# Expert rows turned by VectorE instead of TensorE, and loaded tile by tile from ScalarE's queue

## The reference, cut to what matters

```python
# h: (512, 1024), modulated RMSNorm of the residual stream; 16 experts, two per token
scores = sigmoid(h @ router_w)
# one group of 4 experts by the biased scores, then the top 2 inside it
for e in range(16):
    he = silu(h @ w1[e]) * (h @ w3[e])       # (., 512)
    out = out + gate[:, e:e + 1] * (he @ w2[e])
```

## Time and profile before

| | us |
|---|---|
| median of 3 runs | 1632.22 |
| lowest, highest | 1629.7, 1632.82 |
| the profiled execution, its own time | 1630.77 |
| its span in the profile | 1629.2 |
| first up part starts | 1313.63 |
| last down part over, about | 1601 |

### The profile page before, as it was taken

How to read it: one execution, slowest core, us unless ns; L and a number is a source line. 1 busy time by engine, 2 the same in 40 slices (tenths; PEclk the granted TensorE clock), 3 DMA queues, 4 the chain that set the end, 5 groups by cost and what they waited for, 6 DMA issues and landing times.

```text
span 1629.2 us, 25590 instructions
## 1 busy us (share of the span) xinstructions
PE 1537.2 (94%) x10014; PEld 1045.9 (64%) x10015; DVE 880.8 (54%) x1476; ACT 395.5 (24%) x736; POOL 311.5 (19%) x315
## 2 busy tenths in 40 slices
PE   5999999999999999999999999999999999999792
PEld 2567567567566788887755558888774665555351
DVE  2557848758758898763277765563362312222124
ACT  4342432432432410001133325101201201111112
POOL 0206516417417400000000000000000032222122
PEclk9999999999999999999999999999999989999996
DMA  9803401411411377131101102132637379998984
GB/s 339 330 11 77 126 17 39 129 26 28 128 52 36 147 255 254 60 105 52 52 1 52 52 1 103 54 121 103 241 121 258 132 268 395 376 351 323 395 325 168
DMA packets 110349, 248.61 MB, mean 153 GB/s; under 512 B 5665, under 2 KB 15142, under 8 KB 110274
## 3 DMA queue, kind: packets, MB, share of 16 engines
q1 hardware_dynamic: 86800, 180.60, 30.8%
q0 software_dynamic: 14288, 48.96, 8.4%
q10 hardware_dynamic: 9186, 18.01, 4.1%
HBM read 225.40 MB, written 22.15 MB: 152 GB/s over the span
## 4 chain that ended last, share of the span: by engine, by line
PE 80%; DVE 11%; DMA 4%; issue 1%; ACT 1%; SPq 1%; POOL 0%; ACTq 0%; DVEq 0%; POOLq 0%
PE psum L581 26%; PE psum L1273 9%; PE psum L513 8%; PE psum L1298 5%; PE psum L517 3%; PE psum L527 3%; PE psum L694 2%; PE psum L1089 2%; PE psum L971 2%; PE psum L853 1%; DMA arena<-exp_w_d 1%; PE psum L828 1%; DVE arena L2395 1%; DVE arena L2173 1%; PE psum L819 1%
## 5 line engine op out<-in xcount | busy, mean ns | idle before, releaser
L581 PE MATMUL psum<-arena 128*128 128x256 f32 x2128 | 472.4, 380 | 5.4 <-DVE arena L2063 2.1
L581 PEld LDWEIGHTS psum<-arena 128*128 128x128 f32 x2128 | 400.0, 190 | 73.9 <-issue 17.9
L1273 PE MATMUL psum<-arena 128*32 128x256 f32 x2816 | 165.9, 388 | 1.5 <-issue 1.0
L513 PE MATMUL psum<-arena 128*128 128x512 f32 x320 | 140.4, 592 | 0.0
L1273 PEld LDWEIGHTS psum<-arena 128*32 128x32 f32 x2816 | 89.9, 111 | 62.1 <-issue 7.3
L513 PEld LDWEIGHTS psum<-arena 128*128 128x128 f32 x320 | 59.2, 189 | 69.6 <-issue 69.3
L1991 DVE SCALAR_TENSOR_TENSOR arena<-arena 128x772 f32<-128x772 f32 (+1 forms) x96 | 101.9, 1062 | 3.4
L2773 DVE TENSOR_TENSOR arena<-arena,psum 128x128 f32<-128x128 f32 x44 | 12.7, 289 | 163.8 <-ACT arena L1829 163.8
L2880 POOL TENSOR_TENSOR arena<-arena 128x512 f32<-128x512 f32 x64 | 89.2, 1402 | 17.0 <-ACT arena L1603 16.8
L2941 POOL DMA_DIRECT2D slots<-arena x92 | 50.0, 545 | 196.8 <-DVE arena L2779 176.5
L2864 POOL TENSOR_TENSOR arena<-arena 128x512 f32<-128x512 f32 x32 | 45.1, 1410 | 216.7 <-ACT arena L1541 216.7
(11 more groups left out here) (402 smaller groups left out, 2152.5 us busy)
## 6 DMA issues: line engine op xcount, KB each, us to landing
arena<-exp_w_d SPq DMA_DIRECT2D x48, 2048.0 KB, 16.9
arena<-w_in_d SPq DMA_DIRECT2D x22, 2048.0 KB, 8.0
arena<-ada_w_d POOLq DMA_DIRECT2D x8, 2048.0 KB, 8.6
slots<-arena POOLq DMA_DIRECT2D x1, 9216.0 KB, 27.0
arena<-ada_w_d SPq DMA_DIRECT2D x4, 2048.0 KB, 20.7
arena<-decay_rows ACTq DMA_DIRECT2D x16, 512.0 KB, 6.8
arena<-ssd_proj_d SPq DMA_DIRECT2D x4, 2048.0 KB, 7.8
slots<-arena POOLq DMA_DIRECT2D x92, 64.0 KB, 5.0
```

Source lines behind the costliest of these rows:

```text
L513: ins = mmul(ps[:, 0:T], slot[:, k, m * P:(m + 1) * P], src[:, k, C:NT], start=(k == 0), stop=(k == KD - 1))
L581: ins = mmul(bank((name, at))[:, i * 256:(i + 1) * 256], held[:, k, i * P:(i + 1) * P], passed[:, k, :], start=(p in (1, 5, 6) and i == 0 ...
L1273: ins = mmul(psU[q * R:(q + 1) * R, 0:2 * HF], XT[:, k % 2, k // 2, :], w13[p][:, :, k, q * HF:(q + 1) * HF], start=(k == 0), stop=(k == K ...
```

## The change

Four things change together.

1. The rows of a tile are kept in quarters: row r's channels lie in four partition groups of 32, so that a transpose of 32x32 blocks by VectorE turns them. ScalarE writes `yo` in a reordered channel order, and `up` reads its weights in the matching order. `turn_x` and `turn_h` of TensorE and ScalarE's copy to `heT` go away; VectorE does `take_x` (transpose and scale), `give_x` (shift into `XT`) and `turn_h` (transpose into `heT`).
2. TensorE picks four tiles instead of two, not turned any more: `pick_x(psX, marks)` for tiles 0 and 1, and after `up(0, 0)` `pick_x(psX2, marks2)` for tiles 2 and 3. VectorE makes `marks2` from both choices of a token.
3. The loads of rows move from GpSimd (two tiles in one DMA) to ScalarE's queue: four DMAs of 32 KB a tile, after the previous tile's rows have landed and VectorE has taken a tile. SP loads tile 4, ahead of the last piece of expert 2's weights.
4. TensorE's order in a tile is up(j), down(j-1), and up(j) waits for he_ready itself.

```diff
-            def pick_x():
...
-                for k in range(KD):
+            def pick_x(rows, where):
+
+                for n in range(2):
                     for t in range(TL):
-                        ins = mmul(by_tile[:, :, k % 2, :, k // 2], yo[:, t, k * P:(k + 1) * P],
-                                   marks[:, t, :].rearrange("p (n r) -> p n r", n=2),
-                                   start=(k == 0 and t == 0), stop=(k == KD - 1 and t == TL - 1))
-                ins.then_inc(S_("x_turned"), 1)
-
-            def turn_x():
-                for i in range(DQ // P):
-                    ins = nc.tensor.transpose(psX[:, i * P:(i + 1) * P], xq[:, i * P:(i + 1) * P], ident)
-                ins.then_inc(S_("x_turned"), 1)
+                        for q in range(NQ):
+                            ins = mmul(rows[q * R:(q + 1) * R, n * DQ:(n + 1) * DQ], where[:, t, n * R:(n + 1) * R],
+                                       yo[:, t, q * DQ:(q + 1) * DQ], start=(t == 0), stop=(t == TL - 1))
+                    ins.then_inc(S_("x_picked"), 1)
 
             def up(p, j):
 
+                if not (isinstance(j, int) and j == 0):
+                    pe.wait_ge(S_("he_ready"), j)
+                    pe.sem_inc(S_("pe_passed"), 1)
                 pe.wait_ge(S_("x_ready"), j + 1)
...
-                pe.wait_ge(S_("xq_ready"), j + 2)
-                pe.sem_inc(S_("pe_passed"), 1)
-                turn_x()
-
-            def turn_h(j):
-
-                pe.wait_ge(S_("he_ready"), j + 1)
-                pe.sem_inc(S_("pe_passed"), 1)
-                nc.tensor.transpose(psH[:, 0:P], hg, ident).then_inc(S_("h_turned"), 1)
...
-            pick_x()
+            pick_x(psX, marks)
...
             up(0, 0)
+            pe.wait_ge(S_("marked"), 2)
+            pick_x(psX2, marks2)
...
-            sp.wait_ge(S_("x_sent1"), 16 * TL)
+            for i in range(2):
+                sp.wait_ge(S_("x_sent%d" % i), 16 * TL)
+            sp.wait_ge(S_("x_picked"), 4)
+            R = ROWS_A_TILE
+            for q in range(NQ):
+                sp.dma_start(xrow[q * R:(q + 1) * R, 0:DQ], slots[4 * R:5 * R, q * DQ:(q + 1) * DQ]).then_inc(S_("xrow_in"), 16)
             weights(2, 2, UP[:1])
...
+            def load_x(j):
+
+                for q in range(NQ):
+                    act.dma_start(xrow[q * R:(q + 1) * R, bass.ds((j & (RING - 1)) * DQ, DQ)],
+                                  slots[bass.ds(j * R, R), q * DQ:(q + 1) * DQ]).then_inc(S_("xrow_in"), 16)
...
             with act.Fori(1, n) as j:
-                hidden(j - 1)
+                act.wait_ge(S_("he_ready"), j)
                 gate(j)
-                act.wait_ge(S_("x_turned"), j + 2)
-                x_row(j + 2)
-            hidden(n - 1)
+                act.wait_ge(S_("x_taken"), j + 3)
+                act.wait_ge(S_("xrow_in"), j * (16 * NQ))
+                load_x(j + 4)
+                run(xq, xrow[:, bass.ds(((j + 3) & (RING - 1)) * DQ, DQ)], ACT.Copy).then_inc(S_("xq_ready"), 1)
...
+            def take_x(n, src):
+
+                v.transpose(flat(xs_next), src).then_inc(S_("x_taken"), 1)
+                dve.wait_ge(S_("x_taken"), n + 1)
+                v.tensor_tensor(xs_next, xs_next, A2, ALU.mult).then_inc(S_("x_scaled"), 1)
+
+            def give_x(n):
+
+                dve.wait_ge(S_("x_scaled"), n + 1)
+                v.tensor_tensor(XT, xs_next, B2, ALU.add).then_inc(S_("x_ready"), 1)
...
             with dve.Fori(1, n) as j:
-                hidden(j)
-                modulate_x(j + 2)
+                dve.wait_ge(S_("u_full"), j + 1)
+                give_x(j + 1)
+                gate_up(j)
+                dve.wait_ge(S_("down_full"), j)
+                turn_h(j)
                 out_rows(j)
+                dve.wait_ge(S_("x_ready"), j + 2)
+                dve.wait_ge(S_("xq_ready"), j)
+                take_x(j + 2, xq)
...
             with pool.Fori(0, nb - 1) as b:
-                pool.wait_ge(S_("xq_ready"), b * BATCH + BATCH)
-                pool.wait_ge(S_("xrow_in"), b * 16 + 16)
-                load_x(b + 2)
                 pool.wait_ge(S_("y_ready"), b * BATCH + BATCH + 1)
```

More of the change, by code:

```diff
@@ L292, in build @@
         g2q = alloc(DQ)
-        XT = alloc(DQ // P, NQ, ROWS_A_TILE)
+        XT = alloc(KD, ROWS_A_TILE)
         assert top[0] <= phase_base
@@ L298, in build @@
         yo = alloc(TL, D)
+        xs_next = view(top[0], (KD, ROWS_A_TILE))
         score = alloc(TL, NE)
@@ L324, in build @@
         marks = xq.rearrange("p (t s) -> p t s", t=TL)
-        places = heT.rearrange("p q r -> p (q r)")[:, 0:2 * ROWS_A_TILE]
+        places = heT.rearrange("p q r -> p (q r)")
         ysb = alloc(RING * DQ)
+        marks2, marks_b = [xrow[:, i * DQ:(i + 1) * DQ].rearrange("p (t s) -> p t s", t=TL) for i in range(2)]
         junk2 = xrow
@@ L1322, in expert @@
                 return hi
-            pick_x()
+            pe.wait_ge(S_("x1_normed"), TL)
+            pe.wait_ge(S_("marked"), 1)
+            pick_x(psX, marks)
             pe.wait_ge(S_("tiles_known"), 1)
@@ L1336, in _ @@
             n = bound(NE, 2 * NE)
-            turn_h(n - 1)
             down(0, n - 1)
@@ L1816, in _ @@
             for t in range(TL):
-                run(yo[:, t, :], xr[:, t, :], ACT.Copy, scale=small[:, 24 + t:25 + t]).then_inc(S_("x1_normed"), 1)
+                run(yo[:, t, :].rearrange("p (q j c) -> p j q c", q=NQ, c=ROWS_A_TILE),
+                    xr[:, t, :].rearrange("p (j q c) -> p j q c", q=NQ, c=ROWS_A_TILE), ACT.Copy,
+                    scale=small[:, 24 + t:25 + t]).then_inc(S_("x1_normed"), 1)
             act.wait_ge(S_("tiles_known"), 1)
[L1819 to L1824, removed]
+            n = act.value_load(first_tile_i[0:1, NE:NE + 1], min_val=1, max_val=XTILES - 4 * BATCH)
+            R = ROWS_A_TILE
             def gate(j):
@@ L1856, in _ @@
             run(small[:, 54:55], ones[:, 0:1], ACT.Sqrt)
-            act.wait_ge(S_("xq_ready"), n + 2)
+            act.wait_ge(S_("xq_ready"), n)
+            act.wait_ge(S_("xrow_in"), n * (16 * NQ))
             for t in range(TL):
@@ L2653, in _ @@
             v.memset(twos, 2.0)
-            for i in range(2):
-                v.tensor_tensor_scan(places[:, (1 - i) * ROWS_A_TILE:(2 - i) * ROWS_A_TILE], ones[:, 0:ROWS_A_TILE],
+            for i in range(4):
+                v.tensor_tensor_scan(places[:, i * ROWS_A_TILE:(i + 1) * ROWS_A_TILE], ones[:, 0:ROWS_A_TILE],
                                      ones[:, 0:ROWS_A_TILE], float(i * ROWS_A_TILE - 1), ALU.mult, ALU.add)
@@ L2743, in _ @@
             n_places = [P, TL, 2 * ROWS_A_TILE]
-            v.tensor_tensor(marks, share[:, 0, :].unsqueeze(2).to_broadcast(n_places),
-                            places.unsqueeze(1).to_broadcast(n_places), ALU.is_equal).then_inc(S_("marked"), 1)
-            dve.wait_ge(S_("marked"), 1)
+            near, next_ = [places[:, i * 2 * ROWS_A_TILE:(i + 1) * 2 * ROWS_A_TILE].unsqueeze(1).to_broadcast(n_places)
+                           for i in range(2)]
+            v.tensor_tensor(marks, share[:, 0, :].unsqueeze(2).to_broadcast(n_places), near, ALU.is_equal)\
+                .then_inc(S_("marked"), 1)
+            step(v.tensor_tensor(marks2, share[:, 0, :].unsqueeze(2).to_broadcast(n_places), next_, ALU.is_equal))
+            step(v.tensor_tensor(marks_b, share[:, 1, :].unsqueeze(2).to_broadcast(n_places), next_, ALU.is_equal))
+            v.tensor_tensor(marks2, marks2, marks_b, ALU.add).then_inc(S_("marked"), 1)
+            dve.wait_ge(S_("marked"), 2)
             step(v.tensor_tensor(ra, oh, both(score), ALU.mult))
@@ L2933, in _ @@
             rows = lambda b: slots[bass.ds(b * (BATCH * R), BATCH * R), :]
-            def load_x(b):
-                pool.dma_start(half(xrow, b).rearrange("p (i c) -> p i c", c=DQ),
-                               rows(b).rearrange("(i r) (q c) -> (r q) i c", i=BATCH, c=DQ)).then_inc(S_("xrow_in"), 16)
             def send_y(b):
@@ L2942, in send_y @@
                                    half(ysb, b)[q * R:(q + 1) * R, :].rearrange("r (i c) -> r i c", c=DQ)).then_inc(S_("y_sent"), 16)
-            load_x(1)
             pool.wait_ge(S_("y_ready"), 1)
@@ L2972, in _ @@
             fetch_y(1)
-            pool.wait_ge(S_("xrow_in"), nb * 16)
 def grid_positions():
```

60 lines of the change are left out of this document (27 added, 33 removed).

## The result

The changed kernel takes 1657.05 us (median of 4 runs, 1653.26 to 1657.7), the kernel before 1632.52 us beside it: a ratio of 1.0137, 95% interval 1.0119 to 1.0155. It is slower by 1.4%, where 1628 was forecast and 1612 to 1646 was the range. The profiled execution took 1657.04 us with a span of 1653.8, 24.6 us over the span before.

What follows compares the result with a forecast made beforehand. TensorE's tile period and the weight stream were taken to alternate as bounds. Start -6, tiles and end together -2.5, turn and last stores cancelling, weight waits -1.5, start included: sum -4, forecast 1628 us, range 1612 to 1646.

Steps and rivals of the forecast that it cites:

- the landing term: ScalarE's row loads: beside the weight stream a load lands 4.6 us (4.0 to 5.5) after its issue.
- Floor beside the stream: ScalarE's load loop: registers, three more issues, landing and wake-up make tiles 6.6 us beside the weight stream, against 6.09 before.
- The rows behind 4.6: Profile rows beside a busy stream used for the landing: a 64 KB GpSimd store, 5.0 us; one small ScalarE load, 4.9.
- the gain at the start: Start of the expert stage: tile 1's up matmuls come near 1314.7 instead of 1320.96, gaining 6 us (3 to 8).
- so the pick of tiles 0 and 1 ends 3.7 to 5.8 us after 1299.73: First picking on TensorE: 64 matmuls priced like the up part, ending near 1304.5, up(0) near 1306 instead of 1313.63.
- the stretch of the weight stall: From tile 25 until the weight stall ends: shifts there count for nothing; waits shrink a little, -1.5 us.
- 125 us of stream: Weights for 7 experts at 17.8 us each while 25 tiles run; about 17 tiles meet the stream, 8 do not.
- The second: Rival, ScalarE's queue: later landings or costlier issues, floor 7.1 gives 1640 us, 7.6 gives 1647; chance 0.27.
- The first rival: Row loads land within 3.3 us, tile 5.3, then the weight stream binds: about -24 us, 1608; chance 0.17.
- The Trainium skill's rule on the time of one DMA: Row loads: about 2.0 us plus bytes at 436 GB/s, 2.1 us for 32 KB; cited on the quick-landing rival's side.
- TensorE's free tile: Tile period with nothing else in the way: 5.1 us of matmuls and two handovers of 0.1, about 5.3 us.

Runs made afterwards that it cites:

- second profile: The changed kernel once more, unaltered, as a control among the experiments (the kernel before also got one): 1657.43 us, ratio 1.0151.
- eight DMAs: Against the changed kernel, each row load of ScalarE cut in two: eight DMAs of 16 KB a tile instead of four of 32 KB; 1730.24 us.
- two tiles under way: Against the changed kernel, ScalarE issues tile j+4's loads before waiting for tile j+3's landing, with two semaphores by turns; 1629.47 us, ratio 0.9971 to the kernel before.
- the thin stream: Against the changed kernel, expert weights loaded inside the loop carry an eighth of their columns, same number of DMAs; 1593.81 us.
- the version with the lowest ratio: Against the changed kernel, loads issued before the landing wait (two tiles' loads outstanding), plus 16 matmuls behind the first picking; 1627.19 us, ratio 0.9957.

## Why the prediction was wrong

**The step that failed** is the landing term of "Floor beside the stream: 0.3 + 1.6 + 4.6 + 0.1 = 6.6 us". The mechanism, its place and its other terms were right: 0.38 from landing to issue (forecast 0.4), 1.54 for three issues (1.6). The landing of the last load is not 4.6 us but 5.36 and 5.19 (medians of the two profiles), with a mean of 5.40 in both, so the floor is 7.1 to 7.3. The rows behind 4.6 were a store of GpSimd (5.0) and one load of ScalarE (4.9), and I went below both without a reason. Stores did land sooner in that trace at a DMA share over 0.8 (from 3.5 us), but no load did. The last of four issued in a row has to be taken, not a typical one: over 1344 to 1410 us the median of all loads is 5.0, that of the last of each four, over all tiles beside the stream, 5.36.

**A second term failed**, the gain at the start. By the forecast's own 2 us for 0.1 us of floor, a landing of 5.2 to 5.4 gives 1640 to 1644, still inside the range. Forecast was -6 (3 to 8). It was -9.1 in the first profile, with both pickings at 3.66 us as forecast, but +1.4 in the second and -0.9 to +1.5 in the other experiments. The step "so the pick of tiles 0 and 1 ends 3.7 to 5.8 us after 1299.73" holds for the recorded matmuls and not for their signal.

**The sum.** The two profiles, part by part, against the spans before (24.6 and 25.6 us more):

| | forecast | first profile | second profile |
|---|---|---|---|
| upstream of the picking | 0 | 6.0 | 0.8 |
| picking to tile 1 | -6 | -9.1 | +1.4 |
| tile 1 to 25 | +2.1 | +24.1 | +20.7 |
| tile 25 to 38 | -1.5 | +1.0 | +0.1 |
| tile 38 to 43 | +1.4 | +2.2 | +2.3 |
| behind it | 0 | +0.4 | +0.2 |

In the second profile 17 long tiles at 7.62 instead of 6.6 are 17.3 us of the miss from tile 1 to 25, and seven short ones at 5.43 instead of 5.3 another 0.9; the landing's 0.8 us makes most of the first figure. The first profile's tile 1 is 9.1 us early, and two more of its tiles are long. That the stretch of the weight stall absorbs its share and that the end loses little was right. One step of the forecast's arithmetic was off: 125 us of stream at 6.6 us a tile are 19 tiles and not 17, which would have made its sum 2.6 us higher.

**The rivals.** The second came true: landing 5.2 or more, decided from 6.95 on. (Its sum with a landing of 5.2 is 7.2, not 7.1.) Its price was too low, 1640 at 7.1 and 1647 at 7.6, where 7.1 to 7.3 gave 1657: the gain at the start that it was offset with did not come, and the mean long tile, 7.6, lies above the floor. It is not that more tiles stand beside the stream. The DMA share is over 0.8 for about the same time between tile 1 and 25, 128 us before, 134 and 132 after and 129 with eight DMAs, so longer tiles mean fewer of them beside it: 21, 18 and 12. The first rival was priced wrong too. Its mechanism, made true by two tiles under way, gave 1629 instead of 1608: the stream moved 379 GB/s, not 394, over 243 us instead of 235, and could start only at 1338 instead of 1325. The Trainium skill's rule on the time of one DMA, quoted there, agrees with the 1.8 us of the thin stream and misses the 5.4 us beside the full one; the section gives it for DMAs issued by GpSimd, and these are ScalarE's.

**Where the expected gain went.** TensorE's free tile is 5.3 us, as forecast, with the stream thin in all tiles (1594 us). In the full kernel there are two bounds above it: ScalarE's chain (7.3 us), and behind that the weight stream, which leaves the version with the lowest ratio 0.4% under the kernel before.

**Open.** What delays the signal of the picking by 8 us, and whether it does so outside profiles, is not settled; neither more matmuls behind it nor the lower bound of value_load changed it. Nor is it shown why the landing beside the stream is 5 us for 16 KB and 6 us for 128 KB.

## What to carry to other kernels

A loop that waits for a landing and then issues has a floor: 0.38 us, 0.51 us for each issue after the first, and the landing under load; take the landing from rows with the DMA share at which it will run, of loads if it is a load, the last of a burst, and never below the lowest such row. One transfer more under way removed it here, and one DMA spread over all engines landed sooner than four (6.0 us against 6.9 from the first issue). When a gain rests on TensorE finishing early, look for the signal and not for the matmuls' records. Before pricing a faster tile, price the stream: bytes by the rate of a full stretch, from when its first buffer comes free.

## What the runs showed of the hardware

- A load beside a full DMA share lands 5.0 to 5.4 us after its issue at 16 and 32 KB, 6.0 us at 128 KB; without the stream 1.7 to 1.8 and 2.1 us.
- The same 128 KB with an outermost dimension of 4 went over four engines and took 10.3 us beside the stream and 4.0 alone.
- The first picking's last matmul signalled 7.3 to 7.8 us after its recorded start in eleven of twelve profiles (0.41 us in the twelfth), VectorE waiting all that time.
- The same matmuls upstream (1160 to 1190 us) ran at a granted clock of 0.83 or 1.00 in profiles of one and the same kernel. In the profile with 0.83 the first picking starts 4.1 us later (kernel before) and 5.2 us later (changed kernel); that all of this comes from the clock is not shown.
- With TensorE idle for 8.9 us its granted clock fell from 1.00 to 0.50, and the 64 matmuls that followed took 6.13 us; with matmuls in the gap it stayed at 1.00, and they took 3.8 us.
